# Two transformer layers and a DeltaNet block on one core: the work around the opening, the retention's last pair, the chunk inverses, the end of the scan and the last residual in another order

## The reference, cut to what matters

```python
def first_block(x, ...):                       # two layers, l = 0, 1; x is 512 x 1024, float32
    for l in range(DEPTH):
        z = rmsnorm(x, attn_norm[l]) @ w_in[l]  # 1024 x N_IN, split into the inputs of four branches
        yA = forgetting_attention(qA, kA, vA, fA + forget_bias)       # 8 heads of 64
        yB = dsa_attention(rope(qB), rope(kB), vB, rope(qI), rope(kI), wI)
        yC = head_groupnorm(retention(rope(qC), rope(kC) / 8, vC), ret_norm[l]) * silu(gC)
        yD = sliding_window_gqa(rope(qD), rope(kD), vD, sinks)
        branch = einsum('bsnc,ncd->bsnd', stack([yA, yB, yC, yD]), w_branch[l])
        x = x + sum(sigmoid(gates) * branch, axis=2) @ w_out[l]
        a, b = split(causal_dwconv(rmsnorm(x, ffn_norm[l]) @ w_up[l]))
        x = x + (silu(a) * b) @ w_down[l]       # D_FF = 2816
    return rmsnorm(x, final_norm)

def dsa_attention(...):     # per block of 128 queries
    score = einsum('bqhs,bqh->bqs', relu(qi @ ki.T), wi)
    _, sel = top_k(where(causal, score, neg), 128)   # the 128 best keys of every query
    ...                                              # softmax attention over these keys alone

def second_block(x, c, ctx, ...):              # once; ctx is 256 x 1024 and gives the first states
    sh1, sc1, gt1, sh2, sc2, gt2 = split(silu(c) @ w_ada + b_ada)
    u, z, q, k, v, beta, g = mixer_inputs(modulate(rmsnorm(x, g_pre_mix), sh1, sc1))
    o = bidir_gdn(q, k, v, beta, g, s_f, s_b)  # gated delta rule, chunks of 64, forward + backward
    y_f = einsum('blgc,gcd->blgd', fft2(u).real, w_fourier)           # 4 groups of 128 channels
    y_d = rmsnorm(o, g_gdn) * silu(z)                                 # 4 heads of 128
    x = x + gt1 * rmsnorm(concatenate([y_f, y_d]) @ w_out, g_post_mix)
    h = modulate(rmsnorm(x, g_pre_ffn), sh2, sc2)
    return x + gt2 * rmsnorm(conv_ffn(h, w_up, w_dwc, w_down), g_post_ffn)   # D_FF_2 = 2816

def gated_delta_chunked(...):   # per chunk of 64: decay = exp(gc_i - gc_j), gc the running sum of g
    t_inv = inverse(eye + strict_lower((kb @ kc.T) * decay))
    u_val = t_inv @ vb;  w_key = t_inv @ (kb * exp(gc))
    # scan over chunks: v_new = u - w @ s;  o = (q exp(gc)) @ s + (q k.T * decay) @ v_new;
    #                   s = s * exp(g_last) + k_dec.T @ v_new
```

## Time and profile before

| | us |
|---|---|
| median of three timed runs | 2950.2 |
| the three runs | 2954.25, 2948.92, 2950.2 |
| the profiled execution | 2952.96 |
| its span, from the first to the last instruction | 2951.2 |
| TensorE busy | 2893.0 (98% of the span) |
| GpSimd busy | 1596.6 (54%) |
| VectorE busy | 1561.4 (53%) |
| ScalarE busy | 751.3 (25%) |
| mean granted TensorE clock | 0.993 of full speed |

### The profile page before, as it was taken

How to read it: one execution, slowest core, us unless ns; L and a number is a source line. 1 busy time by engine, 2 the same in 40 slices (tenths; PEclk the granted TensorE clock), 3 DMA queues, 4 the chain that set the end, 5 groups by cost and what they waited for, 6 DMA issues and landing times.

```text
span 2951.2 us, 40986 instructions
## 1 busy us (share of the span) xinstructions
PE 2893.0 (98%) x16283; PEld 2298.9 (78%) x16283; DVE 1561.4 (53%) x3007; ACT 751.3 (25%) x1582; POOL 1596.6 (54%) x1109
## 2 busy tenths in 40 slices
PE   9999999999999999999999999999999998999997
PEld 6777777778888887777778788888888786788886
DVE  6663452356786137633523377873242777766611
ACT  5333331212211033343321122111132322311100
POOL 4444555557555664344555575556534544666664
PEclk9999999999999999999999999999999999999998
DMA  5433444445776555344444456765533001355553
GB/s 212 143 136 138 154 152 164 164 151 200 259 260 235 188 168 181 136 142 144 150 159 169 150 199 237 275 245 188 171 129 136 23 3 52 115 200 199 190 196 136
DMA packets 133135, 490.41 MB, mean 166 GB/s; under 512 B 14912, under 2 KB 14912, under 8 KB 132048
## 3 DMA queue, kind: packets, MB, share of 16 engines
q1 hardware_dynamic: 71024, 262.56, 26.4%
q0 software_dynamic: 60480, 220.23, 20.9%
q10 hardware_dynamic: 1440, 4.99, 0.4%
HBM read 485.59 MB, written 2.13 MB: 165 GB/s over the span
## 4 chain that ended last, share of the span: by engine, by line
PE 73%; issue 11%; POOL 9%; DVE 4%; DMA 2%; ACT 1%; POOLq 0%; SPq 0%; DVEq 0%; ACTq 0%
PE dense L882 19%; PE dense L884 19%; PE dense L883 19%; POOL raw_lo L3017 6%; PE scores L882 2%; PE scores L884 2%; PE scores L883 2%; PE O L1180 1%; POOL weights_hi L3003 1%; DMA weights_hi<-stream 1%; PE scores L1112 1%; PE scores L1166 1%; PE turned L1406 1%; PE O L1146 1%; PE turned L1418 1%
## 5 line engine op out<-in xcount | busy, mean ns | idle before, releaser
L3017 POOL TENSOR_TENSOR raw_lo<-raw,weights_hi 128x1024 fp32r<-128x1024 f32 x420 | 1011.4, 2408 | 43.9 <-DMA weights_hi<-stream 34.7
L3003 POOL DMA_DIRECT2D weights_hi<-stream x420 | 243.9, 581 | 1103.4 <-PE dense L884 1002.8
L882 PE MATMUL dense<-h_hi,weights_hi 128*128 128x512 f32 x2096 | 834.6, 398 | 3.2 <-POOL raw_lo L3017 1.8
L884 PE MATMUL dense<-h_hi,raw_lo 128*128 128x512 f32 x2096 | 817.8, 390 | 0.0
L883 PE MATMUL dense<-h_lo,weights_hi 128*128 128x512 f32 x2096 | 816.2, 389 | 0.0
L882 PEld LDWEIGHTS dense<-h_hi,weights_hi 128*128 128x128 f32 x2096 | 393.6, 188 | 108.5 <-issue 24.2
L884 PEld LDWEIGHTS dense<-h_hi,raw_lo 128*128 128x128 f32 x2096 | 393.4, 188 | 85.0
L883 PEld LDWEIGHTS dense<-h_lo,weights_hi 128*128 128x128 f32 x2096 | 394.0, 188 | 76.8
L882 PE MATMUL dense<-hidden_hi,weights_hi 128*128 128x512 f32 x528 | 205.7, 390 | 0.7 <-POOL raw_lo L3017 0.7
L884 PE MATMUL dense<-hidden_hi,raw_lo 128*128 128x512 f32 x528 | 205.4, 389 | 0.0
L883 PE MATMUL dense<-hidden_lo,weights_hi 128*128 128x512 f32 x528 | 205.4, 389 | 0.0
(11 more groups left out here) (494 smaller groups left out, 4662.2 us busy)
## 6 DMA issues: line engine op xcount, KB each, us to landing
raw<-stream SPq DMA_DIRECT2D x427, 512.0 KB, 3.3
weights_hi<-stream POOLq DMA_DIRECT2D x420, 512.0 KB, 4.4
ada_w<-ada SPq DMA_DIRECT2D x48, 512.0 KB, 5.2
decays<-stream ACTq DMA_DIRECT2D x8, 512.0 KB, 3.9
gates<-f_scratch SPq DMA_DIRECT2D x2, 1536.0 KB, 9.8
x<-x_in SPq DMA_DIRECT2D x2, 1024.0 KB, 7.5
cond_rows<-cond SPq DMA_DIRECT2D x2, 1024.0 KB, 6.5
out<-x SPq DMA_DIRECT2D x4, 512.0 KB, 2.7
```

What stands on the lines that cost most here:

```text
L882: nc.tensor.matmul(to, wh, xh, start=first, stop=False)
L884: return nc.tensor.matmul(to, wl, xh, start=False, stop=final)
L3003: nc.gpsimd.dma_start(w_hi(w), stream[DENSE.items[DENSE.weight_list[w]]]).then_inc(hi_landed[s], 16)
L3017: nc.gpsimd.tensor_tensor(lo, src, hi, ALU.subtract).then_inc(weights_lo, 1)
```

## The change

It reorders work in six places; what is computed stays the same.

- **Opening** (layer 0 only): of the four blocks before the row products two now stand behind them. VectorE norms chunks from misc as soon as the rows are there, in the order given, and scales tok and kIB last; ScalarE copies misc and evacuates tok and kIB after chunk 7.
- **Selection**: the last pair gives one step in segments 2 and 3; the pair before it gets one in segments 0 and 3.
- **Retention**, last pair of each layer: group_scale stands before the decay products; the gated y stays in misc and is rounded and lowered from there.
- **Front of the inverses**: the barred constants get a slot and a transfer of their own, at item ("qkv", 2); rowsum lies in a_mat's place and is made by POOL after each of the last six lows; the bars go straight into dec, and they and the gate factors are computed before z 3's evacuation on VectorE; TensorE's and ScalarE's operations are interleaved one by one, with the row sums in the banks of u 3 and z 3; ed's exponential stands earlier.
- **End of the scan**: inside parts are added in their own step; the last step's state part goes to PSUM and VectorE adds it; the first two output blocks are turned within step 11, before its position products; the first two outputs of the projection take the Fourier blocks first, and four of these stand between the turns; the 24 idle products go; the last Fourier low part is made by VectorE from PSUM; POOL makes the low part of weight W_OUT+2 before the first power. The order of token blocks changes.
- **End**: the last square is taken before the copy; seven idle products stand before the row products; VectorE scales all eight chunks and adds chunks 2, 5, 7 (their scaled value in PSUM), POOL adds 0, 1, 3, 4, 6, and the stores wait for both counts.

The core of the diff (8 columns of indentation are taken off):

```diff
-T_ORDER = (1, 2, 0, 3)
+T_ORDER = (2, 1, 3, 0)
...
-TOPK_SPREAD = ([1, 2, 2, 2, 1, 1], [1, 2, 2, 2, 1, 1], [1, 2, 2, 1, 1, 1], [1, 2, 2, 1, 0, 0])
+TOPK_SPREAD = ([1, 2, 2, 2, 1, 1], [1, 2, 2, 2, 1, 1], [2, 2, 2, 2, 1, 1], [1, 2, 1, 0, 0, 0])
...
+FOURIER_FIRST = ([(j, k) for j in range(2) for k in range(3)] + [(0, 3), (1, 3)] + [(j, k) for j in range(2) for k in range(4, KC)])
...
+END_POOL, END_DVE = (0, 1, 3, 4, 6), (2, 5, 7)
...
-rowsum, rowbar = rows_of("rowsum", ROWSUM_AT, 6), rows_of("rowbar", ROWBAR_AT, 6)
 dec, a_mat = rows_of("gdn_decay", DECAY_AT, 6), rows_of("gdn_a", A_AT, 6)
+rowsum = a_mat
...
+def gated_place(c):
+    return misc[:] if c == PAIRS - 1 else yc
...
+            at = int(CONST2_AT[list(CONSTS2)[3]])
+            sp.dma_start(barred, const2_in[:, at:at + 2 * CHUNK]).then_inc(s_dft, 16)
...
-        sp.wait_ge(x_added, KC + k + 2)
+        sp.wait_ge(x_added, KC + sum(n <= k + 1 for n in END_POOL))
+        if k:
+            sp.wait_ge(end_added, END_ADDED + sum(n <= k + 1 for n in END_DVE))
...
-            fill(4)
+            fill(2)
             pe.wait_ge(s_const, CONST_LANDED)
             norm_rows((l, 1))
+            fill(2)
...
+    def row_products(k):
+        pe.wait_ge(row_summed, k + 1)
+        if k >= 2:
+            pe.wait_ge(row_barred, 2 * GROUPS + k - 1)
+        else:
+            evac_wait((TAIL, "uz"[k], 3))
+        nc.tensor.matmul(ROW_BANK[k % 2], chunk_ones, rowsum[k], start=True, stop=True).then_inc(row_ready, 1)
...
+    pe.wait_ge(l2_var, L2_VAR + 1)
+    pe.wait_ge(s_dft, DFT_LANDED)
+    turn_values(0)
+    turn_values(1)
+    for k in range(4):
+        row_products(k)
+        turn_values(k + 2)
+    row_products(4)
+    turn_keys(0)
+    row_products(5)
+    turn_keys(1)
+    turn_scaled_keys(0)
+    turn_keys(2)
+    turn_scaled_keys(1)
+    for r in range(2):
+        channel_weights(r)
+        turn_keys(r + 3)
+        turn_scaled_keys(r + 2)
+    turn_keys(5)
+    turn_scaled_keys(4)
+    turn_scaled_keys(5)
...
-    pe.wait_ge(row_barred, 4 * GROUPS)
-    evac_wait((TAIL, "u", 3))
+    evac_wait((TAIL, "wf", 0))
+    evac_wait((TAIL, "wf", 1))
     channel_products(0)
...
+    def turn_outputs(first):
+        if first:
+            pe.wait_ge(c_o1, 2 * latent_no(STEPS))
+        for n in (first, first + 1):
+            pe.wait_ge(p_scaled, n + 1)
...
-        else:
+        if s == STEPS - 1:
+            turn_outputs(0)
+        if s > STEPS - 4:
             position_products(3, sum(BY_STEP[x] for x in range(STEPS - 3, s)), BY_STEP[s])
-    for n, t in enumerate(T_ORDER):
-        if n == 2:
-            idle_products(turned[:, 1, :], 24)
-        pe.wait_ge(p_scaled, n + 1)
-        pe.wait_ge(c_o1, 2 * latent_no(STEPS))
-        for h in range(GH):
-            last = nc.tensor.transpose(ROWS_BANK[n][:, h * P:(h + 1) * P], o2[t][:, h * P:(h + 1) * P],
-                                       ident)
-        last.then_inc(p_turned, 1)
-    fill(KC * KC)
+    pe.wait_ge(c_o2, 2 * latent_no(STEPS - 1))
+    fill(4)
+    turn_outputs(2)
+    fill(KC * KC - 4)
...
+    idle_products(turned[:, 1, :], 7)
     norm_rows(5)
...
         l, which = name
-        if which == 1 and k == 2:
+        if which == 1 and k == (2 if l else KC - 1):
+            if l == 0:
+                copy_rows(name)
+                evacuate((l, "tok"))
             evacuate((l, "kIB"))
...
+            act.wait_ge(ab_step, 10)
+            nc.scalar.activation(ed[:], tmp_sc[:, 0:SC], ACT.Exp).then_inc(ab_act, 1)
...
+    copy_values(1)
+    for k in range(4):
+        copy_values(k + 2)
+        decay_exp(k)
...
+        if s == STEPS - 2:
+            act.wait_ge(c_o3, 2)
+        if s == STEPS - 1:
+            act.wait_ge(evacuated[bank_of((TAIL, "pc", 3, 1))], evac_count((TAIL, "pc", 3, 1)))
+        to = turned[:, 1, :] if s == STEPS - 1 else oscan[i]
...
+        if s == STEPS - 3:
+            output_squares(0, 2 * latent_no(STEPS - 2))
+    for n in (2, 3):
+        act.wait_ge(c_o2, 2 * latent_no(STEPS - 1) + n - 1)
+        nc.scalar.activation(SQ4[n], o2[T_ORDER[n]], ACT.Square).then_inc(p_sq, 1)
+    src, _ = result((TAIL, "py", 3))
+    nc.scalar.activation(four_hi[:, 3, :], src, ACT.Copy).then_inc(four_rounded, 1)
...
+        if d == KC - 1:
+            act.wait_ge(square_added, sums_of(5) + d - 2)
+            nc.scalar.activation(square[d % 2], src, ACT.Square, scale=0.5).then_inc(squared, 1)
+            nc.scalar.activation(hT[:, d, :], src, ACT.Copy, scale=0.5).then_inc(done, 1)
+            continue
...
+            dve.wait_ge(*((rows_copied, NORMS[name] + 1) if NORMS[name] else (rows_ready, 1)))
...
+            for k in range(2):
+                normed_chunk(name, k)
+            split_lo_even(name, 0)
+            for k in range(2, 4):
+                normed_chunk(name, k)
+            split_lo_even(name, 2)
+            for k in range(4, 6):
+                normed_chunk(name, k)
+            split_lo_even(name, 4)
+            for k in range(6, KC):
+                normed_chunk(name, k)
+            split_lo_even(name, 6)
+            split_lo_even(name, 7)
+            dve.wait_ge(rows_copied, NORMS[name] + 1)
+            scale_tile(name, 0)
+            scale_tile(name, 1)
+            return
...
+                if s == 0 and c == PAIRS - 1:
+                    group_scale(l, c - 1)
...
-            if s == 0 and c:
+            if s == 0 and 0 < c < PAIRS - 1:
...
+    def end_add(k):
+        part = scores[:, END_DVE.index(k) % 2, :]
+        dve.wait_ge(h_ready, 8 * (NORMS[5] - 2) + k + 1)
+        nc.vector.tensor_tensor(xT[:, k, :], xT[:, k, :], part, ALU.add).then_inc(end_added, 1)
...
+    def keys_factors():
+        dve.wait_ge(s_dft, DFT_LANDED)
+        for d in range(2):
+            for p in range(GROUPS):
+                nc.vector.tensor_tensor(by8(dec[mat_no(d, p)]), over8(barred[:, d * CHUNK:(d + 1) * CHUNK]),
+                                        by_pair(gcum, d, p), ALU.subtract).then_inc(row_barred, 1)
+        dve.wait_ge(l2_ready, 1)
...
+        if c == 2:
+            gate_factors()
+            keys_factors()
+    def decay_rows(k):
+        dve.wait_ge(row_ready, k + 1)
+        nc.vector.tensor_tensor(dec[k], banks[bank_of((TAIL, "uz"[k % 2], 3))], dec[k], ALU.add).then_inc(row_barred, 1)
...
-            if n < 4:
+            if n < 4 or s == STEPS - 1:
                 dve.wait_ge(c_o1, 2 * latent_no(s) + 2)
-            else:
+            if s == STEPS - 1:
+                nc.vector.tensor_tensor(dst[hs, :], dst[hs, :], turned[hs, 1, :], ALU.add).then_inc(c_o3, 1)
+            if n >= 4:
...
+    def last_four_low():
+        dve.wait_ge(four_lo, 3)
+        dve.wait_ge(four_rounded, FOUR_ROUNDED + 4)
+        nc.vector.tensor_tensor(y_lo[:, 3, :], banks[bank_of((TAIL, "py", 3))], four_hi[:, 3, :], ALU.subtract
+                                ).then_inc(four_lo, 1)
     for s in range(STEPS - 4, STEPS - 1):
         new_values(s)
         add_states(s)
-        if s > STEPS - 4:
-            add_inside(s - 1)
+        add_inside(s)
+    output_sums(0)
     new_values(STEPS - 1)
-    add_inside(STEPS - 2)
-    output_sums(0)
+    output_scale(0)
     add_inside(STEPS - 1)
-    output_scale(0)
     output_sums(2)
     output_gate(0)
+    last_four_low()
     output_scale(2)
-    output_gate(2)
+    for n in range(1, TB):
+        output_gate(n)
     for n, t in enumerate(T_ORDER):
...
         dve.sem_inc(hidden_ready, 1)
     norm_var(5)
-    residual(5, 4, KC)
+    for k in range(KC):
+        end_scale(k, hT[:, k, :] if k in END_POOL else scores[:, END_DVE.index(k) % 2, :])
+        if k in END_DVE:
+            end_add(k)
...
+            pool.wait_ge(l2_sums, 4)
+        d, p = divmod(k, GROUPS)
+        nc.gpsimd.tensor_tensor(by8(rowsum[k]), over8(upto_c[:, d * CHUNK:(d + 1) * CHUNK]), by_pair(gg, d, p),
+                                ALU.mult).then_inc(row_summed, 1)
     for w in range(N_LAYER_WEIGHTS + 4, W_OUT):
         if w + 1 < W_OUT:
             issue(w + 1)
         low(w)
+        if w >= W_OUT - 2 * GROUPS:
+            row_sums(w - W_OUT + 2 * GROUPS)
...
     nc.gpsimd.tensor_tensor(l2s[:], l2v[:], minus_half[:], ALU.pow).then_inc(l2_ready, 1)
-    pool.wait_ge(dense_mark, DENSE.item_mark[(TAIL, "z", 3)])
-    for d in range(2):
-        for p in range(GROUPS):
-            nc.gpsimd.tensor_tensor(by8(rowsum[mat_no(d, p)]), over8(upto_c[:, d * CHUNK:(d + 1) * CHUNK]),
-                                    by_pair(gg, d, p), ALU.mult).then_inc(row_summed, 1)
     pool.wait_ge(s_const, CONST2_LANDED)
     def mask(g, lev):
...
     low(W_OUT + 1)
     add_output(10, weights_lo, lows_done(W_OUT + 1))
     pool.wait_ge(c_o3, 6)
+    low(W_OUT + 2)
     output_pow(0)
-    add_output(11, p_pow, 1)
-    pool.wait_ge(c_o3, 8)
     output_pow(1)
-    low(W_OUT + 2)
-    four_low(3)
     issue(W_OUT + 3)
     for d in range(3, KC):
         issue(W_OUT + d + 1)
...
```

(3 more changed lines are left out.)

182 lines of the change are left out of this document (87 added, 95 removed).

## The result

The changed kernel takes 2929.31 us in the median of four runs (2927.53 to 2929.59), against 2951.39 of the kernel before on the same chips (2948.92 to 2954.25): ratio 0.9924, 95% interval 0.9911 to 0.9936. That is 22.1 us less; 24.0 were forecast, and 2929.31 lies in the range. But two terms of the sum failed, by six and by four microseconds in opposite directions, and a loss of clock that no term had came on top.

What follows compares the result with a forecast made beforehand. TensorE, busy 98% of the span, was taken to bound the kernel. Terms 3.2 + 2.8 + 5.1 - 1.1 + 9.8 + 4.2 = 24.0 us came off 2950.2, giving 2926.2 us, range 2917 to 2936.

Steps and rivals of the forecast that it cites:

- Opening: Layer 0's start: earlier row products and reordered norm chunks bring the first score product to 49.8 from 53.14; 3.2 us saved.
- Selection: Pair 4 in both layers: first wait (1.03) goes, second shrinks to 0.65; 2.8 us saved.
- Retention: Last pair, both layers: TensorE's wait of 1.31 goes and that of 1.38 shrinks to 0.1; 5.1 us saved.
- Front: Front of the inverses: GpSimd's pow holds VectorE's bars 8.0 us, TensorE stands 3.25, clock lost; 1.1 us slower.
- Clock: Front of the inverses: a 2.25 us hole kept the clock, 2.70 lost it, so 3.25 loses it; costs 2.6 us.
- Scan end: End of scan: output projection's block 8 starts at 2503.2 instead of 2513.0, with waits of 1.85 and 1.35; 9.8 us saved.
- Rival C: Clock also lost in the scan's end, after 1.85 us of waiting; 3.3 us lost, 2929.5 in all; chance 0.15.
- End: After the last norm: square before copy 0.6, clock kept 1.0, shorter scales and adds 2.6; 4.2 us saved.
- A: Front of the inverses: the pow doesn't hold VectorE, 4.8 us gained instead of 1.1 lost; 2920.3 in all; chance 0.19.
- B: Front of the inverses: the pow holds VectorE but the clock stays; 1.5 us gained, 2923.6 in all; chance 0.15.
- E: Shortened chains weren't the last: opening and scan end give only half; 17.5 us saved, 2932.7 in all; chance 0.12.
- D: Half clock from the scan's end lasts over the output projection, 36 us, 2962 in all, slower than before; chance 0.03.

Runs made afterwards that it cites:

- the run with the late bars: Changed kernel, but VectorE computes the six bars and the keys' factors behind z 3's evacuation, not before it; total 2931.84 us.
- plain order: Changed kernel with the first two outputs of the last projection each taken 0 to 7, without Fourier blocks first; total 2929.75 us.

## Why the prediction was right and where it was wrong

- **Opening**, -3.2, came as -3.6, or about -2.1 against the second profile of the kernel before. Rows at 24.54 and not 25.05 (the 0.5 of the table's first row); the new wait at the first score product, 1.5 forecast, is 1.37; the clock stayed up. The mechanism is right. The size is less sure than it looks: 1.6 of it depend on which profile of the kernel before one subtracts from, and these differ in how long the half clock lasted.
- **Selection**, -2.8, came as -2.7, with the second turn counted in: the first wait went, the second is 0.88, not 0.65. Right.
- **Retention**, -5.1, came as -5.5: the waits were those of the earlier trace rows. Right; ytok's took 0.1 more with it than the view shows, and the one before y_parts 0.1 more than forecast.
- **Front**, +1.1, came as -4.9. The step that failed is "I take 8.0, as every row of another GpSimd operation shows it". The rows were of subtractions and sums that stream whole tiles; the power in question reads 48 columns and takes 8 us over them. The bars beside it ran in 0.68 each, and took 0.46 from the power (8.52 against 8.06 in the earlier trace rows). What was to follow (bank held until 2297.0, a hole of 3.25) followed from that step alone, and the run with the late bars shows what it would have brought: a hole of 2.96 and the clock gone, for 1.5 where 2.6 was forecast. The Trainium skill (SBUF — State Buffer, "Who interferes with whom") has the rule by which I decided. It calls the port pair that VectorE and GpSimd share an exclusive lock, and has a VectorE instruction with two SBUF inputs contend with a GpSimd one that reads SBUF. That the lock is kept for the whole instruction it says of VectorE's two-port modes only; I took it over to the two-input case. The rows disagree with that reading for the power; for the row sum, with 1.44 against 0.68, they agree that there is contention. The measurement decides.
- **Clock.** The forecast tied it to holes: above 2.25 us lost, below kept. The holes of 2.70 and more bear that out, in both profiles of before, in the run with the late bars (2.96) and in plain order (3.73). "Below kept" fails: behind the 1.86 of the scan's end the clock fell in four profiles of eight. And -2.6 in the front was charged to a hole that didn't come, while 3.3 were lost in the inverses behind waits of 0.7 at most, in one profile of ten. A fall with no wait above 0.7 us ahead of it is in seven of the ten profiles, and where it stands changes. Why they come where nothing waits is open.
- **Scan end**, -9.8, came as -10.0, with its two waits. Right. Rival C, the clock lost there too, was at 0.15 and priced at 3.3. In the profile of the result it didn't happen; in four of the eight profiles with this wait it did, and cost 0.5 at the ninth block. So its chance was too low and its price too high.
- **End**, -4.2, came as +0.1: 0.6 for the square, 0.9 for the clock and 2.6 for the additions, all there until the last store's landing, and then 4.4 of waiting for GpSimd where 0.2 stood before. The step that failed is "GpSimd's five adds ... ending 0.15 before": they were held against VectorE's end, and not against the end of the span, to which GpSimd brings 7.2 us of its own. The trace of before shows that drain at 8.27, but no wait hung on it there, and the forecast has no term for it.
- **Rivals.** A came in its mechanism. B fell with the power that was to hold. E is refuted where it spoke of the scan end (10.0 of 9.8), and less clearly for the opening (2.1 to 3.6 of 3.2). D, a half clock over the whole projection, is refuted by all twelve profiles: between 2504 and 2526 none shows it.

The forecast saving was 1.9 too large (24.0 against 22.1), and the forecast time 3.1 too low, the median of before being 1.2 higher than the one it was subtracted from. Behind that stand one error of 6.0, one of 4.3 the other way, 3.3 of clock that no step had, and 1.4 between the profile and the median. The number came out close by luck, because they cancel; the mechanism was right for four of six parts.

## What to carry to other kernels

Work moved to an engine for the last microseconds must be held against what that engine does after it: look at the closing instructions of every engine, not only at those that compute. Don't price contention between VectorE and GpSimd by how long the GpSimd instruction lasts: one of 8 us over 48 columns cost VectorE next to nothing, one of 1.05 us over 512 columns cost it 0.75. That it goes by how much the instruction reads would fit these two, but they differ in their function too, and no run parts the two. And compare two profiles at the place of the edit, by the start of the same instruction: totals here scatter by 2 to 3 us with the clock, as much as most edits are worth.
